# Differential attention with scores and transposes in shared PSUM slots, output one unit late, and squares on GpSimd

## The reference

```python
def diff_attn_core(q, k, v, lam):
    s = jnp.einsum('bqhmd,bkhmd->bhmqk', q, k).astype(F32) * (B_HEAD_DIM ** -0.5)
    p = jax.nn.softmax(s, axis=-1)
    a = p[:, :, 0] - lam * p[:, :, 1]
    return jnp.einsum('bhqk,bkhd->bqhd', a.astype(v.dtype), v)
# behind it: rms_norm(o, subln_w, 1e-5) over the 128 columns of a head, times 1 - lam_init, times silu(z)
```

## Time and profile before

| | |
|---|---|
| median of 3 runs | 1847.0 us (1845.96 to 1847.04) |
| the profiled execution | 1844.38 us, of which the span of the trace is 1842.5 |
| TensorE busy (matmuls) | 1628.7 us, 88% |
| VectorE busy | 926.6 us, 50% |
| ScalarE busy | 541.4 us, 29% |
| GpSimd busy | 162.9 us, 9% |
| the attention stage | 347.9 to 463 us |

### The profile page before, as it was taken

How to read it: one execution, slowest core, us unless ns; L and a number is a source line. 1 busy time by engine, 2 the same in 40 slices (tenths; PEclk the granted TensorE clock), 3 DMA queues, 4 the chain that set the end, 5 groups by cost and what they waited for, 6 DMA issues and landing times.

```text
span 1842.5 us, 22836 instructions
## 1 busy us (share of the span) xinstructions
PE 1628.7 (88%) x8468; PEld 1163.3 (63%) x8468; DVE 926.6 (50%) x1574; ACT 541.4 (29%) x845; POOL 162.9 (9%) x254
## 2 busy tenths in 40 slices
PE   6799999798999999998999998697899988888980
PEld 6588888577788777776788886477344333333330
DVE  3876537665468646566776775655211111111114
ACT  3312221566143354543423652122111010101111
POOL 2000010033011000001110000010000000000002
PEclk9899999789899999999999997796899999999995
DMA  9223353102133310433342011036799999999983
GB/s 362 90 94 120 134 207 116 52 18 81 46 137 123 118 46 1 155 123 120 141 156 92 24 70 46 1 124 274 274 423 423 422 423 423 422 423 422 423 374 142
DMA packets 55794, 353.06 MB, mean 192 GB/s; under 512 B 7408, under 2 KB 7664, under 8 KB 18720
## 3 DMA queue, kind: packets, MB, share of 16 engines
q1 hardware_dynamic: 43056, 306.88, 41.5%
q0 software_dynamic: 12656, 45.07, 6.5%
HBM read 332.26 MB, written 23.59 MB: 193 GB/s over the span
## 4 chain that ended last, share of the span: by engine, by line
PE 59%; DMA 16%; DVE 15%; ACT 4%; issue 3%; SPq 3%; POOL 1%; DVEq 0%; POOLq 0%; ACTq 0%
PE ps L1973 10%; DMA early<-in_experts 10%; PE ps L1975 10%; PE ps L1974 10%; PE ps L2389 6%; PE ps L2161 5%; PE ps L2027 4%; DMA raw<-in_experts 3%; PE ps L2410 3%; SPq L629 2%; PE ps L2370 2%; PE ps L2185 2%; ACT p L888 1%; PE ps L1952 1%; PE ps L2178 1%
## 5 line engine op out<-in xcount | busy, mean ns | idle before, releaser
L1973 PE MATMUL ps<-whi,xth 128*128 128x512 f32 (+1 forms) x768 | 302.2, 394 | 6.5 <-DVE xtl L1546 2.5
L1975 PE MATMUL ps<-whi,xtl 128*128 128x512 f32 (+1 forms) x768 | 298.8, 389 | 0.0
L1974 PE MATMUL ps<-wlo,xth 128*128 128x512 f32 (+1 forms) x768 | 298.5, 389 | 0.0
L1873 DVE TENSOR_TENSOR hid<-hid,ps 128x256 f32<-128x256 f32 x33 | 13.9, 421 | 369.9 <-ACT hid L1128 369.9
L1973 PEld LDWEIGHTS ps<-whi,xth 128*128 128x128 f32 x768 | 146.5, 191 | 36.3 <-DVE xtl L1546 2.8
L1975 PEld LDWEIGHTS ps<-whi,xtl 128*128 128x128 f32 x768 | 146.2, 190 | 29.9
L1974 PEld LDWEIGHTS ps<-wlo,xth 128*128 128x128 f32 x768 | 146.7, 191 | 28.5
L2389 PE MATMUL ps<-early,xe_t 128*64 128x512 f32 x624 | 142.3, 595 | 13.8 <-DMA early<-in_experts 12.6
L1177 DVE TENSOR_TENSOR wlo<-raw,whi 128x2048 fp32r<-128x2048 f32 (+3 forms) x52 | 103.3, 1986 | 75.9 <-ACT whi L817 68.3
L817 ACT ACTIVATE whi<-raw 128x2048 fp32r<-128x2048 f32 (+2 forms) x46 | 85.5, 1858 | 124.0 <-DMA raw<-in_even 33.3
L2389 PE MATMUL ps<-raw,xe_t 128*64 128x512 f32 x432 | 101.0, 600 | 18.6 <-DMA raw<-in_experts 15.7
(11 more groups left out here) (414 smaller groups left out, 2883.5 us busy)
## 6 DMA issues: line engine op xcount, KB each, us to landing
early<-in_experts SPq DMA_DIRECT2D x129, 1024.0 KB, 26.1
raw<-in_experts SPq DMA_DIRECT2D x54, 1024.0 KB, 25.8
raw<-in_ada SPq DMA_DIRECT2D x40, 1024.0 KB, 6.5
ring<-in_experts SPq DMA_DIRECT2D x15, 1024.0 KB, 27.6
raw<-in_even SPq DMA_DIRECT2D x14, 1024.0 KB, 5.1
raw<-in_second SPq DMA_DIRECT2D x10, 1024.0 KB, 5.0
pair_dram<-tmp POOLq DMA_DIRECT2D x66, 128.0 KB, 5.8
early<-in_ada SPq DMA_DIRECT2D x8, 1024.0 KB, 18.3
```

The lines of the kernel that those rows point to most:

```text
L1973: nc.tensor.matmul(v, a[0], b[0], start=first, stop=False)
L1974: nc.tensor.matmul(v, a[0], b[1], start=False, stop=False)
L1975: return nc.tensor.matmul(v, a[1], b[0], start=False, stop=last)
```

## The change

The slots are given out by hand: S(u,0) always in slot 0; S(u,1) and T(u) both in slot 1 for even units and in slot 2 for odd ones, in turn; O in slot 3. TensorE's order in the loop becomes T(u), O(u-1), scores(u+2), and the matmuls of the two halves are issued one for one in turn. ScalarE's order becomes exp(u+1, first), pt(u), exp(u+1, second), output(u-1), and these operations don't wait for their own end. The squares leave ScalarE: GpSimd squares the 128 x 512 output tile of a query tile and adds it up by halving, seven additions, each waiting for the one before. VectorE's order stays; its maxima no longer wait for their own end.

```diff
--- before.py
+++ after.py
@@ -178,15 +178,19 @@
     ada(1, [4])
     for kt in range(4):
         plan.job("mix", "a", kt)
-    for u in range(2):
-        plan.job("S", "even", u, 0)
-        plan.job("S", "even", u, 1)
+    def even_scores(u):
+        for i in range(2):
+            plan.job("S", "even", u, i, slot=i * (1 + u % 2))
+
+    even_scores(0)
+    even_scores(1)
     for u in range(E_UNITS):
-        plan.job("T", "even", u)
+        plan.job("T", "even", u, slot=1 + u % 2)
+        if u:
+            plan.job("O", "even", u - 1, slot=3)
         if u + 2 < E_UNITS:
-            plan.job("S", "even", u + 2, 0)
-            plan.job("S", "even", u + 2, 1)
-        plan.job("O", "even", u)
+            even_scores(u + 2)
+    plan.job("O", "even", E_UNITS - 1, slot=3)
     for kt in range(4, 8):
         plan.job("mix", "b", kt)
     chunk("eout", "o", 0, tiles)
@@ -594,6 +598,7 @@
         def by_feature(x):
             return x.rearrange("p (k n) -> p k n", k=KT)
 
+        halves = slice(0, 64), slice(64, P)
         block = stack.enter_context(nc.Block())
 
 
@@ -686,7 +691,16 @@
                 r = orstd[:, 4 * m:4 * m + 4]
                 pool.wait_ge(s_zin, 16 * (m + 1))
                 nc.gpsimd.tensor_tensor(z, z, subln[:].unsqueeze(1).broadcast_to([P, 4, P]), ALU.mult).then_inc(s_zs, 1)
-                pool.wait_ge(s_oss, 4 * (m + 1))
+                evacuated(pool, "O", "even", 4 * m + 3)
+                sq = tmp[:, 0, 0:512]
+                own(nc.gpsimd.tensor_tensor(sq, o_rows[:, m, :], o_rows[:, m, :], ALU.mult), s_oss)
+                part, n = sq.rearrange("p (h d) -> p h d", d=P), P // 2
+                while n:
+                    own.wait()
+                    to = part[:, :, 0:n] if n > 1 else oss[:, 4 * m:4 * m + 4].unsqueeze(2)
+                    own(nc.gpsimd.tensor_tensor(to, part[:, :, 0:n], part[:, :, n:2 * n], ALU.add), s_oss)
+                    n //= 2
+                own.wait()
                 powers(r, oss[:, 4 * m:4 * m + 4], P, SUBLN_EPS, s_ors)
                 pool.wait_ge(s_ors, m + 1)
                 nc.gpsimd.tensor_tensor(o, o, r.unsqueeze(2).broadcast_to([P, 4, P]), ALU.mult).then_inc(s_orow, 1)
@@ -876,34 +890,38 @@
                 v = filled(act, "mix", "a", kt)
                 own(nc.scalar.activation(xth[:, kt, :], v[:, 0:TOK], ACT.Copy), s_xhi)
 
-            def exps(u):
-                m = u // 4
-                for i, pbuf in ((0, p0[:, u % 3, 0:keys(m)]), (1, p1[:, u % 2, 0:keys(m)])):
-                    if i == 0 and u >= 3:
-                        filled(act, "T", "even", u - 3)
-                    if i == 1 and u >= 2:
-                        act.wait_ge(s_comb, u - 1)
-                    act.wait_ge(s_nb, 2 * u + i + 1)
-                    st = soft[:, u % 4, :]
-                    own(nc.scalar.activation(pbuf, slot(("S", "even", u, i))[:, 0:keys(m)], ACT.Exp,
-                                         bias=st[:, 2 + i:3 + i],
-                                         accum_out=st[:, 4 + i:5 + i]), ev("S", "even", u, i))
-
-            exps(0)
-            exps(1)
+            def exp_half(u, i):
+                n = keys(u // 4)
+                if i == 0 and u >= 3:
+                    filled(act, "T", "even", u - 3)
+                if i == 1 and u >= 2:
+                    act.wait_ge(s_comb, u - 1)
+                act.wait_ge(s_nb, 2 * u + i + 1)
+                st = soft[:, u % 4, :]
+                pbuf = p1[:, u % 2, 0:n] if i else p0[:, u % 3, 0:n]
+                own.free(nc.scalar.activation(pbuf, slot(("S", "even", u, i))[:, 0:n], ACT.Exp, bias=st[:, 2 + i:3 + i],
+                                              accum_out=st[:, 4 + i:5 + i]), ev("S", "even", u, i))
+
+            def heads_out(u):
+                v = filled(act, "O", "even", u)
+                o = o_rows[:, u // 4, P * (u % 4):P * (u % 4) + P]
+                own.free(nc.scalar.activation(o, v[:, 0:P], ACT.Copy, scale=soft[:, u % 4, 6:7]), ev("O", "even", u))
+
+            exp_half(0, 0)
+            exp_half(0, 1)
             for u in range(E_UNITS):
+                if u + 1 < E_UNITS:
+                    exp_half(u + 1, 0)
                 v = filled(act, "T", "even", u)
                 if u >= 2:
                     filled(act, "O", "even", u - 2)
                 n = keys(u // 4)
-                own(nc.scalar.activation(pt[:, u % 2, 0:n], v[:, 0:n], ACT.Copy), ev("T", "even", u))
-                if u + 2 < E_UNITS:
-                    exps(u + 2)
-                v = filled(act, "O", "even", u)
-                o = o_rows[:, u // 4, P * (u % 4):P * (u % 4) + P]
-                own(nc.scalar.activation(o, v[:, 0:P], ACT.Copy, scale=soft[:, u % 4, 6:7]), ev("O", "even", u))
-                own.free(nc.scalar.activation(junk[:, P * (u % 4):P * (u % 4) + P], o, ACT.Square,
-                                              accum_out=oss[:, u:u + 1]), s_oss)
+                own.free(nc.scalar.activation(pt[:, u % 2, 0:n], v[:, 0:n], ACT.Copy), ev("T", "even", u))
+                if u + 1 < E_UNITS:
+                    exp_half(u + 1, 1)
+                if u:
+                    heads_out(u - 1)
+            heads_out(E_UNITS - 1)
             for kt in range(4, 8):
                 v = filled(act, "mix", "b", kt)
                 own(nc.scalar.activation(xth[:, kt, :], v[:, 0:TOK], ACT.Copy), s_xhi)
@@ -1363,7 +1381,7 @@
                 n = keys(u // 4)
                 for i in range(2):
                     v = filled(dve, "S", "even", u, i)
-                    own(nc.vector.tensor_reduce(st[:, 2 + i:3 + i], v[:, 0:n], AX, ALU.max, negate=True), s_nb)
+                    own.free(nc.vector.tensor_reduce(st[:, 2 + i:3 + i], v[:, 0:n], AX, ALU.max, negate=True), s_nb)
 
             def combine(u):
 
@@ -2082,32 +2100,38 @@
                 m, h = u // 4, u % 4
                 if m == 0:
                     pe.wait_ge(s_qk_lo, 2 * h + 2)
-                at_ = slice(P * m, P * m + P)
-                for i in range(2):
-                    f = slice(64 * i, 64 * i + 64)
-                    v = begin("S", "even", u, i)
-                    for lo in range(0, keys(m), 512):
-                        hi = min(lo + 512, keys(m))
-                        mm = three(v[:, lo:hi], (qt_h[f, h, at_], qt_l[f, h, at_]), (kt_h[f, h, lo:hi], kt_l[f, h, lo:hi]),
-                                   True, True)
-                    end(mm, "S", "even", u, i)
-
-            scores(0)
-            scores(1)
-            for u in range(E_UNITS):
-                m, h = u // 4, u % 4
-                pe.wait_ge(s_comb, u + 1)
-                turn(("T", "even", u), [p0[:, u % 3, P * n:P * n + P] for n in range(keys(m) // P)],
-                     [P * n for n in range(keys(m) // P)])
-                if u + 2 < E_UNITS:
-                    scores(u + 2)
+                n, at_ = keys(m), slice(P * m, P * m + P)
+                two = [begin("S", "even", u, i) for i in range(2)]
+                for lo in range(0, n, 512):
+                    hi = min(lo + 512, n)
+                    for k, (a, b) in enumerate(((0, 0), (0, 1), (1, 0))):
+                        for i, v in enumerate(two):
+                            f = halves[i]
+                            mm = nc.tensor.matmul(v[:, lo:hi], (qt_h, qt_l)[a][f, h, at_], (kt_h, kt_l)[b][f, h, lo:hi],
+                                                  start=k == 0, stop=k == 2)
+                            if hi == n and k == 2:
+                                end(mm, "S", "even", u, i)
+
+            def out(u):
+                h, last = u % 4, keys(u // 4) // P - 1
                 v = begin("O", "even", u)
                 evacuated(pe, "T", "even", u)
-                last = keys(m) // P - 1
                 for n in range(last + 1):
                     mm = nc.tensor.matmul(v[:, 0:P], pt[:, u % 2, P * n:P * n + P], vb[:, n, P * h:P * h + P],
                                           start=n == 0, stop=n == last)
                 end(mm, "O", "even", u)
+
+            scores(0)
+            scores(1)
+            for u in range(E_UNITS):
+                pe.wait_ge(s_comb, u + 1)
+                cols = [P * n for n in range(keys(u // 4) // P)]
+                turn(("T", "even", u), [p0[:, u % 3, at_:at_ + P] for at_ in cols], cols)
+                if u:
+                    out(u - 1)
+                if u + 2 < E_UNITS:
+                    scores(u + 2)
+            out(E_UNITS - 1)
             pe.wait_ge(s_post, NT)
             for kt in range(4, 8):
                 turn(("mix", "b", kt), [o_rows[:, m, P * (kt - 4):P * (kt - 4) + P] for m in tiles], [P * m for m in tiles])
@@ -2143,8 +2167,6 @@
             permute(("rope", "kr", 0), kr_t[:, CTX:TOK])
 
             banks = ((0, 512), (512, TOK))
-
-            halves = slice(0, 64), slice(64, P)
 
             def attend_pairs(stage, units, score, pbuf, pts, v_of, n, between=None):
```

## The result

The change makes the kernel slower by 0.9%: 1864.13 us (median of 4 runs, 1859.09 to 1865.06) against 1846.91 beside it, ratio 1.0089 (95%: 1.007 to 1.0107). The forecast was 1871, range 1860 to 1886. The profiled execution took 1864.48 us, span 1862.8; predicted was 1869.1.

The account below looks back on a forecast made before the run. Bound: a closed ring of both exps, combine and maximum, without matmuls. Start to unit 8 4.5, ring and clock 0.27 + 9.8 + 0.7, end -0.2, tail 4.6, collisions 5 make 24.7 over 1847.0: 1871, range 1860 to 1886.

Parts of the forecast that it names:

- rival C: Squares on GpSimd and combines on VectorE pass each other without collisions: 5 us less, 1866; chance 17%.
- exp(0) to exp(2): Stage start: scores(1) shares slot 0 with scores(0) and waits for its exp; exp(2) at 360.0 against 357.12, +2.9.
- 256-key turns, unit 8: Early units: pt adds 0.27 us in each of five turns, 1.3; scores not hidden at unit 8, +0.3.
- ring, 14 turns and the first: 768-key units: pt between the exps lengthens exp, exp, combine, maximum by 0.70 us, 14 times 9.8; first turn 0.27.
- collisions: GpSimd's square delays VectorE's combine in each of five tiles, 1.0 us a tile: +5, ends 0 and 18.
- end: From exp(23) to the last output copy: 10.2 us against 10.37, so -0.2, ends -1 and +1.5.
- tail: After the last output copy: GpSimd's square and seven additions take 5.0 us, every engine waiting: +4.6, ends 3 and 7.
- Rival A: TensorE, 94% busy, was the real bound, and shorter scores make the kernel faster: 1838; chance 3%.
- Rival B: TensorE's new idle time holds its clock at 1.2 GHz through the 768-key units: 18 us more, 1889; chance 10%.
- Halves alternately: Alternating the score halves' matmuls on TensorE is worth nothing by itself; with both slots free they already run at once.
- The signs: Profile signs: pt in the chain, first exps 5.4 to 5.6 us apart, TensorE about 70% busy at clock 1.00, GpSimd 5 us.
- Rival D: GpSimd's square and both postprocessing products delay each combine they meet, 2.6 us a tile: +8 more, 1880; chance 14%.

Follow-up runs that it names:

- e4: Kernel before the change, only exps, pt and maxima no longer wait for their own end: 1841.34 us, ratio 0.9975 to the kernel before.
- e3: Changed kernel with exps, pt, output copies and maxima waiting for their own end again: 1873.68 us, ratio 1.0146 to the kernel before.
- e7: Changed kernel, but the score matmuls of the second half follow those of the first: 1860.21 us, ratio 1.0083 to the kernel before.
- e5: Changed kernel with squares back on ScalarE and pt after both exps, slots still shared, halves alternated: ratio 1.0056 to the kernel before.
- e8: e4 with the first maximum of unit u+2 ahead of combine(u+1) in VectorE's list: 1848.62 us, ratio 1.0016 to the kernel before.
- e1: Changed kernel with the squares and their sums back on ScalarE: 1853.45 us, ratio 1.0043 to the kernel before.
- e10: e6 with pt back between the two exps: ratio 1.0052 to the kernel before.
- e6: e5 with a slot each for both score halves, T and O, and halves issued one after the other: ratio 0.9992 to the kernel before.
- e2: Kernel before the change with only the squares moved to GpSimd: 1852.95 us, ratio 1.0041 to the kernel before.
- e9: Changed kernel with the last query tile's four squares on ScalarE again: 1857.7 us, ratio 1.0071 to the kernel before.

## Why the prediction was right, and where its sizes were off

The forecast's mechanism was the one that ran, in its four large parts: pt in the ring, the longer start, GpSimd's tail, the caught combines. The time alone would not say so: 1864 lies nearer to the 1866 of rival C (no collisions) than to 1871, and it is the timelines that show the collisions. Its sum was 7.5 us too high against the medians (24.7 against 17.2), and 6.3 in the stage (24.7 against 18.2 + 0.2 ahead of it):

| step | predicted | measured |
|---|---|---|
| first exp(0) | +0.2 | +0.21 |
| exp(0) to exp(2) | +2.7 | +1.92 |
| 256-key turns, unit 8 | +1.6 | about 0 |
| ring, 14 turns and the first | +10.1 | 14 x 0.42 = +5.9 |
| clock | +0.7 | about +1.5 |
| collisions | +5 | 0.67 among the 256-key units, then 3 x 0.67 + 0.88: +3.6 |
| end | -0.2 | +1.02 |
| tail | +4.6 | +4.45 |

*The ring, the step that was mis-sized.* pt costs exactly the 0.70 that the earlier trace rows gave (5.22 - 4.52, e4). What was off is the half sentence in brackets behind it, that the exps' waits give "a little back" and were entered at nothing: they give 0.28 a turn (4.80 - 4.52, e4). An exp followed its predecessor after 1.02 and does so after 0.89 now; VectorE's reciprocal follows the end of the second exp's read by 0.09 where it was 0.20 (the read ends 445.72, the reciprocal starts 445.81). 14 times 0.28 is 3.9 of the 6.3. The same saving explains the 256-key turns, where it was forgotten too: pt's 0.27 and the 0.28 cancel (2.89 now and 2.88 before, 2.60 in e4). With the waits kept (e3) the start is 7.04, near the 7.2 forecast, and the 256-key turns are 3.2 to 3.3, a little over the forecast's 3.15 (2.88 + 0.27).

*Rival A* (TensorE the bound) is out: a pair of scores that keeps TensorE 0.6 less is worth nothing (e7), and no matmul is in the ring of an ordinary turn of the change or of e4. e5 and e8 show that it is near: where the scores come to be waited for, it decides at once.

*Rival B* (the clock) happened in part and cost little. Over 382 to 459 the mean clock is 0.83, and the transposes take 1.43 and the output 2.63 in places. But TensorE has idle time now and the slower work mostly fits into it. Two turns show it: at 415.30 VectorE had waited 1.17 for the scores (a turn of 6.36), at 392.38 it had waited 0.37 (a turn of 5.56). The Trainium skill ("TensorE: Matmul & The Clock Gate", section "A second HAM failure mode: psum-queue depth-cycling") describes a kernel that cycles through PSUM, pauses briefly between its groups of matmuls and swings between the two clock levels. The swing is in this trace (0.57 and 1.00 in neighbouring stretches) and not in the trace before (1.00 throughout 400 to 448). But pauses in each turn are not enough for it here: e1, with the same order and TensorE busy only 33 of the 48 us of 400 to 448, has a mean clock of 0.97 there. What tips it stays open; in the changed kernel both turns that waited for the scores (5.56 and 6.36) follow directly on a turn with a collision, but e10 and e6, without squares on GpSimd, have such turns too. The 18 us of rival B did not come: they assumed the low level in every turn.

VectorE's two waits for the scores in the changed kernel:

```profile
392.38 1.82 DVE L1384 TENSOR_REDUCE stat<-ps 128x1 f32<-128x768 f32 x2 [0.37 <-PE ps L2110]
...
415.30 1.82 DVE L1384 TENSOR_REDUCE stat<-ps 128x1 f32<-128x768 f32 x2 [1.17 <-PE ps L2110]
```

TensorE around it: transposes and output before the pair of scores at the lower clock (1.54 for six, 2.77 for twelve, where the earlier trace rows have 0.82 and 1.58).

```profile
408.96 1.54 PE L2045 MATMUL ps<-ident,p 128*128 128x128 f32 x6 [1.93 <-DVE p L1396]
410.29 2.77 PE L2120 MATMUL ps<-vb,pt 128*128 128x128 f32 x12
```

*Rivals C and D* (no collisions, more collisions). There is one in each of the five tiles, at the place where it was expected, and in the changed kernel only the square makes a turn longer; the products of the postprocessing delay none there (in e4 and e6, where the turn is shorter, one of them does). Each collision costs 0.67 to 0.88, not the 1.0 taken. e1 removes them all, e2 brings them into the kernel before.

*Halves alternately* was "worth nothing by itself": true of the time (e7). The reason given, that the two halves run at once anyway where both slots are free, holds for the 256-key rows it was read from and not for 768 keys, where the second half of e7 begins 0.57 after the first (1.90 for the pair against 1.31). With e5 it is also seen what alternating does when the scores are waited for: the pair ends after 1.3, but neither half before.

*The end* came out 1.2 above the forecast. The last two outputs take 2.77 and 2.23, that is at the lower clock, where 1.5 and 1.6 were entered. In e1, e2 and e9 the same stretch takes 8.7 to 8.9, near the 9.3 worked out for full clock; in the kernel before, e4 and e6 it has slow outputs as well. So which level the end meets isn't set by this change, and why it differs from kernel to kernel stays open. With e1's end the sum would have been 2.5 lower.

*The tail* came out near its 4.6 partly by luck: the square took 1.04 where 1.28, the time of a product of two tensors, was entered, and the idle 0.29 behind the power, which nobody had foreseen, made up for it.

*The signs* that the prediction named came out in part. The chain with pt in the ring came as said, and so did the stretched combine once in four units and the tail (4.60 for the eight operations, said was 5). The first exps were 5.22 apart and not 5.4 to 5.6, TensorE was busy 78% at a clock of 0.84 and not about 70% at 1.00, and the stretched combine took 1.69 and not over 2. Rival D was also priced for two operations (2.6 a tile, 1880) where it names three; by the prediction's own 1.3 each it would have been 1885 or 1886.

## What to carry to other kernels

Find the closed ring first (here exp, exp, combine, maximum), and price an edit by what it puts into that ring or takes out: a copy that cost nothing behind the second exp costs its full 0.70 us between the two. An operation in such a ring that waits for its own end without need costs some 0.1 us for the next one and again for its reader, and dropping these waits was the only part of the change that paid in these runs (e4, ratio 0.9975). When a term is set down as "gives a little back", put a number on it and multiply it by the turns.

## What was not expected of the hardware

- The wait for an operation's own end costs its neighbours more than it seems: exp to exp 1.02 with, 0.89 without; exp to pt 1.02 and 0.90 (405.16 to 406.18 in e3, 443.14 to 444.04 in the changed kernel).
- GpSimd and VectorE hold each other up by most of an operation and in both directions. A combine lost 0.67, an operation on one element per partition 0.88, and GpSimd's first addition (256 elements) took 1.32 us in the mean over four tiles of the stage (382 to 459) against 0.72 at the end, where VectorE was idle.

```profile
L701 POOL TENSOR_TENSOR tmp<-tmp 128x256 f32<-128x256 f32 x4 | 5.3, 1319 | 0.6
```
- Matmuls of 64 rows in the two halves of the array share more of their time when the two are issued alternately: twelve (768 keys) in 1.31 us, against 1.90 one half after the other with both slots free (e7, 455.30). For six (256 keys) both orders take 1.01.
